# Two transformer blocks on one core: the second block's mixer in another order, the layer loop written out

## The reference

```python
x = rmsnorm(x, norm_final)                       # end of first_block
ada = silu(c) @ w_ada + b_ada                    # shift1, scale1, gate1, shift2, scale2, gate2
h = rms_norm(x, norm1_g) * (1 + scale1) + shift1
qa, ka, va, qb, kb, vb = split(h @ w_in)         # 512, 128, 128, 512, 512, 512 columns
o_a = windowed_gqa(qa, ka, va, sink, t5_table)   # 8 heads of 64, band of 128, bias, sink
o_b = neighbourhood_attention(qb, kb, vb, rpb)   # 8 heads of 64, 2-D windows, bias
mixed = concat(rms_norm(o_a, out_norm_a), rms_norm(o_b, out_norm_b))
x = x + gate1 * (mixed @ w_out)
h2 = rms_norm(x, norm2_g) * (1 + scale2) + shift2
x = x + gate2 * peer(h2)                         # 128 x 128 product-key experts
return rms_norm(x, final_g)
```

## Time and profile before

| | us |
|---|---|
| median of 3 runs | 1878.51 |
| runs | 1873.74, 1878.69, 1878.51 |
| the profiled execution, its time | 1877.37 |
| the profiled execution, its span | 1876.1 |
| PE busy in the span | 1744.8 (93%) |
| DVE / ACT busy | 1328.0 / 916.6 |
| granted TensorE clock, mean | 0.961 |

### The profile page before, as it was taken

One profiled execution on the slowest core, in us unless ns is written; L12 is line 12 of the kernel. 1 busy time (PEld: TensorE's weight loads), 2 busy tenths in 40 slices (PEclk: granted clock), 3 DMA queues, 4 the chain that ended last, 5 costly groups with the idle time before them and its releaser, 6 DMA issues.

```text
span 1876.1 us, 33631 instructions
## 1 busy us (share of the span) xinstructions
PE 1744.8 (93%) x11630; PEld 1601.4 (85%) x11630; DVE 1328.0 (71%) x2304; ACT 916.6 (49%) x1602; POOL 62.3 (3%) x116
## 2 busy tenths in 40 slices
PE   5999899997999899969876999999999999999997
PEld 5999798887899798858765999999999988888885
DVE  4875677776866578766545499998888866666665
ACT  4445344443354344443433455557777755445543
POOL 0000011000000012100000000000000000000000
PEclk9999899998999899988857999999999999999999
DMA  5655477753444598763203545555444445555553
GB/s 190 207 189 197 152 283 267 268 187 113 164 157 158 179 357 288 252 213 113 90 12 119 185 146 179 179 179 169 135 136 139 144 157 193 194 194 190 191 194 140
DMA packets 92611, 337.61 MB, mean 180 GB/s; under 512 B 10985, under 2 KB 11145, under 8 KB 92065
## 3 DMA queue, kind: packets, MB, share of 16 engines
q1 hardware_dynamic: 80064, 289.06, 45.5%
q0 software_dynamic: 11472, 43.03, 6.8%
q10 hardware_dynamic: 976, 4.19, 0.6%
HBM read 334.10 MB, written 6.07 MB: 181 GB/s over the span
## 4 chain that ended last, share of the span: by engine, by line
PE 41%; DVE 11%; issue 2%; ACT 2%; DVEq 0%; ACTq 0%
PE bank L197 12%; PE bank L198 12%; PE bank L199 12%; DVE Z L84 6%; PE bank L1370 3%; DVE w_lo L178 3%; PE bank L416 1%; DVE xn L84 1%; PE bank L251 1%; DVE st L84 1%; PE bank L361 1%; PE bank L1197 0%; ACT w_hi L176 0%; ACT xn L84 0%; DVE rows L84 0%
## 5 line engine op out<-in xcount | busy, mean ns | idle before, releaser
L178 DVE TENSOR_TENSOR w_lo<-raw,w_hi 128x1024 fp32r<-128x1024 f32 x546 | 661.4, 1221 | 210.4 <-ACT w_hi L176 209.3
L197 PE MATMUL bank<-u_hi,w_hi 128*128 128x256 f32 x2416 | 700.8, 290 | 10.9 <-DVE cw L84 3.2
L176 ACT ACTIVATE w_hi<-raw 128x1024 fp32r<-128x1024 f32 x546 | 574.2, 1052 | 244.4 <-PE bank L199 211.9
L198 PE MATMUL bank<-u_lo,w_hi 128*128 128x256 f32 x2416 | 687.5, 285 | 0.0
L199 PE MATMUL bank<-u_hi,w_lo 128*128 128x256 f32 x2416 | 687.1, 284 | 0.0
L197 PEld LDWEIGHTS bank<-u_hi,w_hi 128*128 128x128 f32 x2416 | 467.2, 193 | 22.8 <-issue 14.2
L198 PEld LDWEIGHTS bank<-u_lo,w_hi 128*128 128x128 f32 x2416 | 467.5, 194 | 4.7 <-issue 2.4
L199 PEld LDWEIGHTS bank<-u_hi,w_lo 128*128 128x128 f32 x2416 | 467.0, 193 | 0.0
L197 PE MATMUL bank<-w_hi,a_hi 128*128 128x512 f32 x768 | 299.6, 390 | 1.8 <-DVE a_lo L1447 1.8
L198 PE MATMUL bank<-w_lo,a_hi 128*128 128x512 f32 x768 | 299.5, 390 | 0.0
L199 PE MATMUL bank<-w_hi,a_lo 128*128 128x512 f32 x768 | 298.8, 389 | 0.0
(11 more groups left out here) (226 smaller groups left out, 1709.8 us busy)
## 6 DMA issues: line engine op xcount, KB each, us to landing
raw<-stream SPq DMA_DIRECT2D x546, 512.0 KB, 3.3
gate<-w_ada POOLq DMA_DIRECT2D x48, 512.0 KB, 3.9
space<-b_ada POOLq DMA_DIRECT2D x6, 512.0 KB, 4.6
ada<-ada_rows POOLq DMA_DIRECT2D x6, 512.0 KB, 9.6
t_rows<-t_by_distance POOLq DMA_DIRECT2D x8, 256.0 KB, 3.7
gains_b<-gains POOLq DMA_DIRECT2D x1, 2048.0 KB, 12.9
rpb_rows<-rpb_pad POOLq DMA_DIRECT2D x8, 224.0 KB, 3.9
gains<-gains POOLq DMA_DIRECT2D x3, 512.0 KB, 5.4
```

The costliest lines, as they stand in the source:

```text
L176: nc.scalar.activation(w_hi[:, s, :], raw[:, s, :], ACT.Copy).then_inc(s_hi, 1)
L178: nc.vector.tensor_tensor(w_lo[:, s, :], raw[:, s, :], w_hi[:, s, :].bitcast(F32), ALU.subtract).then_inc(s_split, 1)
L197: M.matmul(o, lh, rh, start=start, stop=False, skip_group_check=True)
L198: M.matmul(o, lh, rl, start=False, stop=False, skip_group_check=True)
```

## The change

1. The layer loop is a Python loop, so the body is issued twice in the program, and `restart_lines` and the meetings are gone. The last layer has no `row_scales`.
2. `piece_a` and `down` mark each of the four banks at its last matmul, and each add of `add_to_x` waits for its own bank.
3. Entry: x times the final gain is taken first; ACT squares both x and that product; one root serves both norms (`both`, from r(x) and EPS). The first norm's own root and the scaling of x itself come after the transposes. Scale and shift are applied behind the transposes, when features lie on partitions (`modulated_to_u`): four groups of four transposes, and per 128 features one DVE `tensor_scalar` from PSUM into `hT`, one ACT copy to `u_hi`, one DVE subtraction to `u_lo`. The first piece waits for each of its eight row groups apart (`ready`).
4. `ada` is read as four columns of 128 x 8 (`load_column`, elements of 4 bytes) and one broadcast row (gate 1) in place of six broadcast rows.
5. kb and qb pieces alternate. The two attentions are four generators (`unit_a`, `unit_b`, each for tile 0 and 1), placed by the table `beside`. The branch norm is no longer applied before w_out: only the gain is (`og`), and the row scale is applied with the gate when the projection comes back (`add_branch`). w_out runs as four pieces for branch A, with steps of B between them, and four for branch B.
6. After w_out: as 3, and x is parked after `modulated_to_u`.

```diff
-        with nc.Fori(0, LAYERS, engines=compute) as layer:
-            at["quads"] = layer * (N_LAYER // RING)
-            restart_lines()
+        for layer in range(LAYERS):
...
-                m = VE.go((mark,), V.tensor_tensor, cols, cols, bank[b][:, :], ALU.add)
+                m = VE.go((bank_marks[tt][n],), V.tensor_tensor, cols, cols, bank[b][:, :], ALU.add)
...
+        def load_column(j, g, done):
+            G.dma_start(acol[:, j, :], ada_dram[g:g + 1, :].rearrange("a (k p) -> p (a k)", p=P),
+                        allow_slow_non_contiguous=True).then_inc(done, 16)
...
-        for g in range(ADA_GROUPS):
-            G.dma_start(ada[:, g, :], ada_dram[g:g + 1, :].partition_broadcast(P).rearrange(
-                "p a n -> p (a n)")).then_inc(s_ada1 if g < 2 else s_ada2, 16)
+        G.dma_start(gate1[:, :], ada_dram[2:3, :].partition_broadcast(P).rearrange(
+            "p a n -> p (a n)")).then_inc(s_ada2, 16)
+        for j, g in ((2, 3), (3, 4)):
+            load_column(j, g, s_ada2)
...
+        def modulated_to_u(src, marks, scaled, j):
...
+            for g in range(KD // 2):
+                b = (6, 7, 0, 1)[g]
+                i = transposes(b, [src[:, tt, k * P:(k + 1) * P] for k in (2 * g, 2 * g + 1) for tt in range(NT)],
+                               marks)
+                for e in range(2):
+                    k = 2 * g + e
+                    m = VE.go((i, *(ready[k - 4] if k >= 4 else ())), V.tensor_scalar, hT[:, k % 4, :],
+                              bank[b][:, e * T:(e + 1) * T], acol[:, 2 * j + 1, k:k + 1],
+                              acol[:, 2 * j, k:k + 1], ALU.mult, ALU.add)
+                    m1 = AC.go((m,), S.activation, u_hi[:, k, :], hT[:, k % 4, :], ACT.Copy)
...
+        both = root(st, NT, m)
+        for tt in range(NT):
+            m = VE.go((both, *g_marks[tt]), V.tensor_scalar, xn[:, tt, :], xn[:, tt, :],
+                      st[:, 3, tt:tt + 1], None, ALU.mult)
+        h_ready = modulated_to_u(xn, (m,), scaled, 0)
+        U = (u_hi, u_lo)
+        r1_mark = root(st2, NT, m1)
...
+        main, a0, a1, b0, b1 = project(), unit_a(0), unit_a(1), unit_b(0), unit_b(1)
+        beside = {3: (a0,), 4: (a1,), 5: (a0,), 6: (a1,), 7: (a0, a1), 8: (a0, a1), 9: (a0,),
+                  10: (a1, a0), 11: (a1, a0), 12: (a1, b0), 13: (a0, a1), 14: (a1, b0), 15: (b1, b0),
+                  16: (b1,), 17: (b0, b1)}
...
+        outs = out_pieces(0)
+        for side in ((b0,), (b1,), (b0,), (b1, b0)):
+            next(outs)
+            for u in side:
+                next(u, None)
+        r_a = branch_scales(0)
+        next(b1, None)
+        add_branch(0, r_a, 0)
+        next(b0, None)
+        add_branch(0, r_a, 1)
+        for u in (b1, b0, b1):
+            run(u)
+        run(out_pieces(1))
+        r_b = branch_scales(1)
+        scaled = column_scale(1, ada_rest)
+        for tt in range(NT):
+            add_branch(1, r_b, tt)
```

More of the change, by code:

```diff
@@ L163, in build @@
         at = {"piece": 0, "quads": 0}
+        bank_marks = [[None, None], [None, None]]
         def dyn(k):
@@ L205, in piece_b @@
                 for k in range(kt):
+                    if ready is not None:
+                        PE.wait(*ready[k])
                     col = (part * kt + k) * P
@@ L226, in run @@
                 pass
-        ss_marks, norm_late, scales = [], [], []
+        ss_marks, norm_late, scales = [], [], [None]
         free = {}
@@ L1108, in side2 @@
-        def side2():
-            for _ in range(7):
-                yield
-            va_part()
-            chains = [chain(0, buf), chain(1, buf2)]
-            for n in range(1000):
-                for c in range(2):
-                    if c == 0 or n >= LAG:
-                        if chains[c] is not None and next(chains[c], "end") == "end":
-                            chains[c] = None
-                if chains == [None, None]:
-                    return
-                yield
-        VE.wait((s_sink, 16))
@@ L1124, in build, with branch_scales @@
-        weave(main2(), side2())
-        PE.wait(*(m for marks in got["mix"] for m in marks))
-        acc = acc_banks()
-        for k in range(KD):
-            m = piece_a(acc, U, (k,), D, k == 0, k == KD - 1)
-        last = m
-        x_marks = [[None, None], [None, None]]
-        for tt in range(NT):
+        def branch_scales(kind):
+            marks = [got["squares", kind, tt] for tt in range(NT)]
+            m = VE.go(marks, V.tensor_scalar, sst[:, kind, 1, :], sst[:, kind, 0, :], 1.0 / W, EPS,
+                      ALU.mult, ALU.add)
+            return root(sst[:, kind, :, :], NT, m)
@@ new lines, in build @@
+        for tt in range(NT):
+            m = squares(x, space_lo, 5, x_marks, tt)
+        m = VE.go((m,), V.tensor_tensor, st[:, 0, :], st[:, 5, :], st[:, 6, :], ALU.add)
+        ss_marks[:] = [m]
+        m = inverse_root(st, D, NT)
+        for tt in range(NT):
+            m = VE.go((m,), V.tensor_scalar, xn[:, tt, :], x[:, tt, :], st[:, 3, tt:tt + 1], None, ALU.mult)
+        h2_ready = modulated_to_u(xn, (m,), scaled, 1)
+        AC.wait(x_marks[NT - 1][1])
+        S.dma_start(x_dram.rearrange("t p d -> p t d"), x[:, :, :]).then_inc(s_park, 16)
@@ L1182, in build @@
             take(b)
-            piece_b([bank[b][:, 0:T]], *U)
+            piece_b([bank[b][:, 0:T]], *U, ready=h2_ready if f == 0 else None)
             m = piece_b([bank[b][:, T:2 * T]], *U)
```

387 lines of the change are left out of this document (254 added, 133 removed).

## The result

| | before | after |
|---|---|---|
| median, us | 1878.60 (1873.74 to 1879.32, 4 runs) | 1835.64 (1834.51 to 1837.86, 4 runs) |
| span of the profiled execution | 1876.1 | 1833.2 |

The ratio is 0.9778, with a 95% interval of 0.9759 to 0.9798: 43 us less.

What follows compares the result with a forecast made beforehand. PE is full nearly everywhere, so gains come only where it stands or clocks low, in the second block's mixer and at layer ends. 25.8 + 4.8 - 1.5 + 1.2 = 30.3 us off 1877.37 gave 1847.1, said as 1848, range 1840 to 1859.

Steps and rivals of the forecast that it cites:

- Layer loop: Between the layers: DVE's waits of 3.93 and 0.93 us for meeting and jump both go, 4.8 us won.
- the 1.5 taken back for the clock: First pieces after the layer boundary: the shorter standstill leaves the clock low, 1.5 us lost, between 0 and 2.9.
- The layers: Up to the second layer's last matmul: 4.5 us gain predicted, with 0 for pieces behind the two inner norms.
- Adds by bank: Adds inside the layers: waiting per bank saves 0.4 us at each of three places, 1.2 us in all.
- Entry: Start of the second block's mixer: first piece 7.2 us earlier, of which 5.6 us are left at the fourth piece.
- The mixer: Fourth piece to last of vb: PE work of 71.8 us plus waits of 0.5, 2.1 and 0.3; projection ends at 932.0.
- The bare tail: Behind w_out for A: a bare stretch of 16 us, not 55, second product 7.06 us; w_out for B starts at 966.3.
- What the reordering wins: Mixer: B's softmax of both tiles runs under pieces; w_out for A with its companions takes 18.3 us, to 950.3.
- Crowded queues: Mixer, rival at 20%: ACT and DVE queues hold each other up, five of fifteen steps waiting 2.1 us each; about 1858.
- B still last: Mixer, rival at 5%: B's steps do not get ahead, most of the 55 us stays, some 14 us won; 1864.
- The clogged stream: Weight stream, rival at 3%: 4-byte column loads keep it off the DMA engines, PE loses 19.7 us twice; 1887.
- The tail at full clock: Bare tail, rival at 10%: product and transposes keep the full clock, 3.5 + 2.8 us less; about 1842.

Runs made afterwards that it cites:

- b_layers: The kernel before with only the layer loop's two turns written out: 1869.89 us, ratio 0.9964 to before.
- a_again: The kernel after, unchanged, measured again later: 1837.04 us, ratio 0.9788 to before.
- b_heads: The kernel before with one table changed, scores of attention A taking head pairs in the order 0, 4, 2, 6: 1872.19 us against 1876.69, ratio 0.9986.
- a_columns2: The kernel after with each scale and shift column load made four times, extra loads to places of their own, no waits between: 1836.69 us.

## Why the prediction was right, and where not

- **Layer loop: right** in size (4.8, b_layers), and right in the 1.5 taken back for the clock: the kernel after lost 1.5 us in the second layer's first pieces, and twelve of the thirteen profiles without the loop and without added matmuls have 3.0 to 3.7 us at the low clock there.
- **The layers, a second step that failed: the clock behind the two norms inside them was put at nothing.** The profiled execution gained 9.3 us in the layers for 4.5 predicted. Of the 4.8 more, 3.3 are these pieces and 1.0 the norms' bare stretches, which became 0.7 and 1.1 us shorter where 0.4 each had been named. Part of this is luck of the execution: the nine kernels with the same code up to the entry reach it between 830.64 and 837.25 us, the one shown first of all. In a_again the gain in the layers is 6.6, so some 2 us of the 4.8 stand for the kernel. Why the clock stays up behind one norm and not the other is open; b_heads, with the layers of before, has 2.9 and 0 us at the low clock behind the two norms and 5.9 behind the boundary.
- **Adds by bank: right** (1.7 for 1.2).
- **Entry: right** as a whole and by its steps: 5.5 for 5.6 (the terms of DVE's queue add up to 856.8 and not 857.3, and the fourth piece began at 862.66 before and not 862.9), rescaling 0.7 each, a wait at the fourth piece of 2.7 where some 1.6 was named, because PE was ready sooner.
- **The mixer: the step that failed is the price of the scores.** Fourth piece to the last of vb was 68.8 us, predicted 74.7. I priced four steps of A at 1.99, the row of before in its old order of heads, though the change alters that order, and B's four at 2.0, their time of before in a stretch at a mean clock of 0.56. All eight take 1.14: 6.8 us less. With them the sentence fell that from 857 to 922 the change brings no less work. The waits were 0.6 us shorter than named (1.8 for 2.1 at the tenth piece), and against both stand 1.7 us that had been put at nothing: the fourth piece at the low clock behind its wait. Together that is 5.7 of the 5.9.
- **The bare tail: right in place, 1.5 too long.** The second product took 5.63, partly at the full clock, where 7.06 was assumed. The rest was right: 18.1 for 18.3 up to it, 26.2 for 26.3 from w_out for B to the transposes, 14.4 for 14.3 to the fourth query piece.
- **What the reordering wins.** The sum came out nearly right, the reason only in part. I put the win on B's place under pieces. The runs show two effects that share it: with the roots out of the chain, B's place is worth about 10 us; with them in, and with the place of w_out for A, twice that.
- **The rivals.** Crowded queues: one such wait, not five. B still last: no. The clogged stream: no (a_columns2). The tail at full clock: little of it, 1.4 us of 3.5 in the product and none of 2.8 in w_out for B, which took 13.75.

The misses add up: scores 5.9 and layers 4.8 less, tail 1.5 less, 0.3 elsewhere: 12.5 for 1848 - 1835.6 = 12.4. By the profile of a_again the sum is 2.7 us smaller, all of it in the layers. All had one sign, and the two ends of the range had been worked out from clock and queues, not from the prices of steps.

## What to carry over

When a change alters the order of operands, read the price of a step from a row in the new order, or bound it from both sides; and look at the clock of a row before using its duration. A short chain on the path costs its own length and what the clock takes from the matmuls behind it: take it off the path first (a row scale can wait until after the product), and fill what stays with work of any kind. Work that is put off must be put where the engine's queue is idle by the trace; the mask behind the fifth piece gave back most of what it won, behind the twelfth nothing.

## What was not expected of the hardware

- 64-row matmuls in the two halves of the rows run side by side: they start in pairs, 0.01 us apart, one pair every 0.22 us. In the same half one starts every 0.22 us. Each record lasts 376 ns either way.
- Added matmuls of no use took 5 to 7 us off a kernel of 1836 us; the mean granted clock rose from 0.980 to 0.991.
- In nine of the eleven profiles in which PE waits 2.68 us ahead of the fourth piece, the clock fell within that piece, which took 4.4 to 5.5 us in place of 3.04.
- Column loads of 4-byte elements take 8 us for 4 KB, and 32 packets each; twelve more of them cost nothing that can be measured.
